# First weights of experts 4 to 30 in 4 MB transfers with 32 KB runs, another issue order, and the last second weight in the first-weight ring

## The reference

```python
for e in range(N_EXPERTS):                       # 32 experts
    z = jnp.einsum('bsd,df->bsf', h, w1[e]) + b1[e]      # w1[e]: 1024 x 2048 float32, 8 MB
    glu = jnp.minimum(z[..., 0::2], SWIGLU_LIMIT)
    lin = jnp.clip(z[..., 1::2], -SWIGLU_LIMIT, SWIGLU_LIMIT)
    act = glu * jax.nn.sigmoid(SWIGLU_ALPHA * glu) * (lin + 1.0)
    out = out + combine[..., e:e + 1] * (jnp.einsum('bsf,fd->bsd', act, w2[e]) + b2[e])   # w2[e]: 1024 x 1024, 4 MB
```

## Time and profile before

| | |
|---|---|
| median of 3 executions | 1123.79 us (1121.34 to 1123.82) |
| profiled execution | 1121.74 us, its span 1120.0 us |
| mean granted clock of TensorE | 0.985 of 2.4 GHz |
| TensorE matmuls busy | 1050.3 us (94%) |
| moved from HBM | 427.98 MB, 384 GB/s over the span |
| queue of SP's transfers | 40180 packets, 427.34 MB, 91.3% of 16 engines' span |
| chain of waits | PE 67%, DMA 30% |

### The profile page before, as it was taken

How to read it: one execution, slowest core, us unless ns; L and a number is a source line. 1 busy time by engine, 2 the same in 40 slices (tenths; PEclk the granted TensorE clock), 3 DMA queues, 4 the chain that set the end, 5 groups by cost and what they waited for, 6 DMA issues and landing times.

```text
span 1120.0 us, 11962 instructions
## 1 busy us (share of the span) xinstructions
PE 1050.3 (94%) x4658; PEld 406.7 (36%) x4658; DVE 288.7 (26%) x694; ACT 181.6 (16%) x323; POOL 17.4 (2%) x20
## 2 busy tenths in 40 slices
PE   8899998999999999998999999898989898989895
PEld 7548644333333333332333323232323232323231
DVE  3446345122222222121221212221212131312122
ACT  3411133111111111111111111111111111111102
POOL 0320000000000000000000000000000000000000
PEclk8999998999999999999999999999999999999998
DMA  9773592999899999999999999999999999999984
GB/s 303 218 273 150 224 411 102 367 427 425 369 430 425 427 427 430 430 427 428 430 430 428 427 430 430 428 427 428 430 430 427 428 430 430 427 427 430 428 365 189
DMA packets 41833, 430.89 MB, mean 385 GB/s; under 512 B 5856, under 2 KB 7444, under 8 KB 17012
## 3 DMA queue, kind: packets, MB, share of 16 engines
q1 hardware_dynamic: 40180, 427.34, 91.3%
q10 hardware_dynamic: 1216, 1.70, 0.8%
q0 software_dynamic: 416, 1.57, 0.4%
HBM read 427.98 MB, written 2.62 MB: 384 GB/s over the span
## 4 chain that ended last, share of the span: by engine, by line
PE 67%; DMA 30%; DVE 2%; SPq 1%; issue 1%; ACT 0%; DVEq 0%; ACTq 0%
DMA w1r<-w_mlp 28%; PE ps L1097 27%; PE ps L1126 13%; PE ps L1142 5%; PE ps L909 5%; PE ps L921 4%; PE ps L1071 3%; PE ps L1003 1%; PE ps L1032 1%; PE ps L1079 1%; PE ps L1105 1%; DMA w2r<-w_mlp 1%; PE ps L1150 1%; DMA arena<-rel_bias 0%; PE ps L1088 0%
## 5 line engine op out<-in xcount | busy, mean ns | idle before, releaser
L1097 PE MATMUL ps<-w1r,arena 128*64 128x512 f32 x2048 | 475.2, 598 | 20.4 <-DMA w1r<-w_mlp 20.4
L1126 PE MATMUL ps<-w2r,arena 128*64 128x512 f32 x1024 | 230.1, 598 | 24.8 <-DMA w2r<-w_mlp 24.8
L1097 PEld LDWEIGHTS ps<-w1r,arena 128*64 128x64 f32 x2048 | 135.2, 136 | 280.9 <-issue 236.2
L1126 PEld LDWEIGHTS ps<-w2r,arena 128*64 128x64 f32 x1024 | 71.9, 137 | 172.5 <-issue 128.5
L830 DVE TENSOR_TENSOR acc<-ps,acc 128x512 f32<-128x512 f32 x64 | 41.2, 686 | 206.3 <-PE ps L1142 206.3
L822 DVE TENSOR_TENSOR arena<-arena 128x512 f32<-128x512 f32 x32 | 22.2, 693 | 199.1 <-ACT arena L509 199.0
L518 ACT ACTIVATE arena<-ps 64x512 f32<-64x512 f32 x32 | 18.9, 592 | 328.9 <-PE ps L1126 328.9
L788 DVE TENSOR_SCALAR sel_z<-small 96x64 bf16 (+1 forms) x32 | 6.1, 190 | 233.6 <-PE ps L1097 233.6
L1142 PE MATMUL ps<-arena 128*128 128x512 f32 x128 | 63.2, 618 | 1.3 <-ACT arena L520 1.3
L1071 PE MATMUL ps<-h,arena 128*64 128x512 f32 x256 | 62.1, 607 | 1.8 <-DVE arena L790 1.8
L909 PE MATMUL ps<-w1r,h 128*128 128x512 f32 x128 | 56.9, 603 | 0.0
(11 more groups left out here) (205 smaller groups left out, 544.0 us busy)
## 6 DMA issues: line engine op xcount, KB each, us to landing
w1r<-w_mlp SPq DMA_DIRECT2D x127, 2048.0 KB, 32.7
w2r<-w_mlp SPq DMA_DIRECT2D x64, 2048.0 KB, 23.4
w1r<-w_in SPq DMA_DIRECT2D x7, 2048.0 KB, 21.3
w1r<-w_out SPq DMA_DIRECT2D x2, 2048.0 KB, 10.0
w1r<-w_mlp SPq DMA_DIRECT2D x2, 1024.0 KB, 5.6
rel_table<-arena ACTq DMA_DIRECT2D x1, 1536.0 KB
acc<-x SPq DMA_DIRECT2D x2, 512.0 KB, 4.4
arena<-rel_table POOLq DMA_DIRECT2D x1, 1024.0 KB, 12.1
```

The lines of the kernel that those rows point to most:

```text
L1097: ins = mm(ps[64 * c:64 * c + 64, 2 * par + n, :], hgT[:, par, k % 4, 64 * (k // 4):64 * (k // 4) + 64], w1r[:, 8 * par + k, at:at + 512], ...
L1126: ins = mm(ps[at:at + 64, 4 + c, :], actT[:, k % 4, 64 * (k // 4):64 * (k // 4) + 64], w2r[:, k // 2, col:col + 512], start=False, stop=(k ...
```

## The change

- `HALVES = 14`, four semaphores `w1_half` and three `w2_last` are added.
- `next_half` replaces `next_w1` for experts 4 to 30: two transfers of 4 MB, four ring rows each, 32 KB in one piece per partition in HBM and in the ring (`w1_c`; the assignment of weight rows to partitions and ring rows is the same as before). The first waits until rows 0 to 3 of the expert two back are used, the second for rows 4 to 7. On TensorE, `z_rows` of these experts waits at k = 0 and k = 4 instead of at every even k. Experts 0 to 3 and 31 keep the 2 MB transfers.
- The order in `rest_of_sweep` becomes: w1 of 2, w1 of 3; then for m = 2, 3, 4: w2 of 2m-3, w1 of 2m, w2 of 2m-2, w1 of 2m+1; then w2 of 7; then for m = 5 to 14: w2 of 2m-2, w1 of 2m, w2 of 2m-1, w1 of 2m+1, with the pass of m = 15 written out, w1 of 31 in quarters, w2 of 30, and `last_w2`.
- `last_w2` puts w2 of expert 31 into ring rows 0 to 3 (expert 30's, rows 0 to 3) and not into `w2r`: one transfer of 2 MB as soon as rows 0 and 1 are used, and two of 1 MB (8 KB per partition) as soon as rows 2 and 3 are. `down(31)` waits for them at k = 0, 4 and 6.
- The final gain and the result move to ring rows 4 and 5.
- On TensorE steps 2 and 3 are written out; the loop runs over m = 2 to 14.
- Further sweeps get one more wait and other counts; they don't run here.

```diff
+            def next_half(base, e, par):
+                for h in range(2):
+                    sp.wait_ge(w1_used, 8 * base + (8 * (e - 2) + 4 * h + 4))
+                    at = 8 * par + 4 * h
+                    sp.dma_start(w1r[:, at:at + 4, :].rearrange("p a f -> p (a f)"), w1_c[e, h]).then_inc(w1_half[2 * par + h], 16)
+
+            def last_w2(base):
+                sp.wait_ge(w1_used, 8 * base + 8 * (NE - 2) + 2)
+                sp.dma_start(w1r[:, 0:2, :].rearrange("p a f -> p (a f)"), w2_v[NE - 1, 0]).then_inc(w2_last[0], 16)
+                sp.wait_ge(w1_used, 8 * base + 8 * (NE - 2) + 4)
+                for i in range(2):
+                    sp.dma_start(w1r[:, 2 + i, :], w2_v[NE - 1, 1, :, 2048 * i:2048 * i + 2048]).then_inc(w2_last[1 + i], 16)
+
                 next_w1(base, 2, 0)
                 next_w1(base, 3, 1)
-                next_w2(base, 1)
-                next_w1(base, 4, 0, range(0, 2))
-                next_w2(base, 2)
-                next_w1(base, 4, 0, range(2, 4))
-                next_w1(base, 5, 1, range(0, 1))
-                next_w2(base, 3)
-                next_w1(base, 5, 1, range(1, 4))
-                next_w2(base, 4)
-                with sp.Fori(3, NE // 2) as m:
-                    next_w1(base, 2 * m, 0)
+                with sp.Fori(2, 5) as m:
+                    next_w2(base, 2 * m - 3)
+                    next_half(base, 2 * m, 0)
+                    next_w2(base, 2 * m - 2)
+                    next_half(base, 2 * m + 1, 1)
+                next_w2(base, 7)
+                with sp.Fori(5, NE // 2 - 1) as m:
+                    next_w2(base, 2 * m - 2)
+                    next_half(base, 2 * m, 0)
                     next_w2(base, 2 * m - 1)
-                    next_w1(base, 2 * m + 1, 1)
-                    next_w2(base, 2 * m)
-                next_w2(base, NE - 1)
+                    next_half(base, 2 * m + 1, 1)
+                next_w2(base, NE - 4)
+                next_half(base, NE - 2, 0)
+                next_w2(base, NE - 3)
+                next_w1(base, NE - 1, 1)
+                next_w2(base, NE - 2)
+                last_w2(base)
...
-                if k % 2 == 0:
+                if halves and k % 4 == 0:
+                    pe.wait_ge(w1_half[2 * par + k // 4], 16 * lap)
+                if not halves and k % 2 == 0:
                     pe.wait_ge(w1_in[4 * par + k // 2], 16 * lap)
...
-                    if k % 4 == 0:
-                        pe.wait_ge(w2_in[k // 4], 16 * base + 16 * (e + 1))
+                    if last and k in (0, 4, 6):
+                        pe.wait_ge(w2_last[max(0, k // 2 - 1)], hb + 16)
+                    if not last and k % 4 == 0:
+                        pe.wait_ge(w2_in[k // 4], 16 * wb + 16 * (e + 1))
...
-                                 w2r[:, k // 2, col:col + 512], start=False, stop=(k == 7))
+                                 (w1r if last else w2r)[:, k // 2, col:col + 512], start=False, stop=(k == 7))
```

More of the change, by code:

```diff
@@ L32 @@
 SLOTS = 64
+HALVES = 14
 SWEEPS = S // SLOTS
@@ L170, in hybrid_block @@
         actT = carve(arena, 5376, [4, P])
-        fgb = w1r[:, 0, 0:1024]
-        res = w1r[:, 1:2, :].rearrange("p a (t d) -> p (a t) d", t=TT)
+        fgb = w1r[:, 4, 0:1024]
+        res = w1r[:, 5:6, :].rearrange("p a (t d) -> p (a t) d", t=TT)
         ps = ctx.enter_context(nc.psum_tensor("ps", [P, 8, 512], F32))
@@ L205, in hybrid_block @@
         w1_in = [sem(f"w1_in{i}") for i in range(8)]
+        w1_half = [sem(f"w1_half{i}") for i in range(4)]
         w1_first = sem("w1_first")
         w2_in = [sem(f"w2_in{i}") for i in range(2)]
+        w2_last = [sem(f"w2_last{i}") for i in range(3)]
         w1_used = sem("w1_used"); w2_used = sem("w2_used")
@@ L222, in hybrid_block @@
         w1_v = w_mlp1[0].rearrange("e (c p i a) f -> e c i p (a f)", c=2, p=P, i=2)
+        w1_c = w_mlp1[0].rearrange("e (c p j) f -> e c p (j f)", c=2, p=P)
         w2_v = w_mlp2[0].rearrange("e (c p j) d -> e c p (j d)", c=2, p=P)
@@ L328, in _ @@
                     base = sp.snap(r * NE)
+                    sp.wait_ge(w2_used, 4 * base)
                     next_w1(base, 0, 0)
@@ L1088, in z_bias, with z_rows @@
                         mm(ps[64 * c:64 * c + 64, 2 * par + n, :], sel_z[:, par, :], bias3[:, at:at + 512], start=True, stop=False)
-            def z_rows(base, lap, k, par):
-                if k % 2 == 0:
+            def z_rows(base, lap, k, par, halves):
+                if halves and k % 4 == 0:
+                    pe.wait_ge(w1_half[2 * par + k // 4], 16 * lap)
+                if not halves and k % 2 == 0:
                     pe.wait_ge(w1_in[4 * par + k // 2], 16 * lap)
@@ L1109, in hgT_until, with down @@
                 return min(e + 3, NE) if isinstance(e, int) else e + 3
-            def down(base, e, par, free=True, tail=False):
+            def down(base, hb, wb, e, par, free=True, tail=False, last=False):
                 pe.wait_ge(actT_sb, base + e + 1)
@@ L1151, in gates_T, with step @@
                 ins.then_inc(gT_tr, 1)
-            def step(base, hb, m, par, first=False, last=False):
+            def step(base, hb, wb, rb, m, par, first=False, last=False):
                 e = 2 * m + par
-                lap = hb + m + 1
+                halves = not (isinstance(m, int) and (m < 2 or last and par == 1))
+                if halves:
+                    lap = rb * (HALVES - par) + m - 1
+                else:
+                    lap = rb * (2 + par) + min(m + 1, 3)
                 head, tail = first and par == 0, last and par == 1
@@ L1160, in step @@
                 z_bias(base, e, par, free=not first)
-                z_rows(base, lap, 0, par)
-                z_rows(base, lap, 1, par)
+                z_rows(base, lap, 0, par, halves)
+                z_rows(base, lap, 1, par, halves)
                 if not tail:
@@ L1166, in step @@
                     gather(base, e + 1, 1 - par)
-                z_rows(base, lap, 2, par)
+                z_rows(base, lap, 2, par, halves)
                 if par == 1 and not first:
                     scatter(base, hb, m - 1, 0)
-                z_rows(base, lap, 3, par)
+                z_rows(base, lap, 3, par, halves)
                 if not tail:
                     gather_T(base, e + 1)
-                z_rows(base, lap, 4, par)
+                z_rows(base, lap, 4, par, halves)
                 if par == 1 and not first:
                     scatter(base, hb, m - 1, 1)
-                z_rows(base, lap, 5, par)
+                z_rows(base, lap, 5, par, halves)
                 if not head:
                     act_T(base, e - 1)
-                z_rows(base, lap, 6, par)
+                z_rows(base, lap, 6, par, halves)
                 if par == 1:
                     gates_T(base, hb, m)
-                z_rows(base, lap, 7, par)
+                z_rows(base, lap, 7, par, halves)
                 if not head:
@@ L1185, in step, with sweep @@
                         pe.wait_ge(added[1], hb + m)
-                    down(base, e - 1, 1 - par, free=not (first and par == 1), tail=tail)
-            def sweep(base, hb, start=False):
+                    down(base, hb, wb, e - 1, 1 - par, free=not (first and par == 1), tail=tail)
+            def sweep(base, hb, wb, rb, start=False):
                 gather(base, 0, 0)
@@ L1194, in sweep @@
                 gather_T(base, 0)
[L1195 to L1199, removed]
+                step(base, hb, wb, rb, 0, 0, first=True)
+                step(base, hb, wb, rb, 0, 1, first=True)
+                step(base, hb, wb, rb, 1, 0)
+                step(base, hb, wb, rb, 1, 1)
+                with pe.Fori(2, NE // 2 - 1) as m:
+                    step(base, hb, wb, rb, m, 0)
+                    step(base, hb, wb, rb, m, 1)
                 m = NE // 2 - 1
-                step(base, hb, m, 0)
-                step(base, hb, m, 1, last=True)
-                down(base, NE - 1, 1)
+                step(base, hb, wb, rb, m, 0)
+                step(base, hb, wb, rb, m, 1, last=True)
+                down(base, hb, wb, NE - 1, 1, last=True)
                 scatter(base, hb, NE // 2 - 1, 0)
                 scatter(base, hb, NE // 2 - 1, 1, bank=0)
-            sweep(0, 0, start=True)
+            sweep(0, 0, 0, 0, start=True)
             pe.wait_ge(sweeps_ready, 1)
@@ L1211, in _ @@
                 with pe.Fori(1, n) as r:
-                    sweep(pe.snap(r * NE), pe.snap(r * (NE // 2)))
+                    sweep(pe.snap(r * NE), pe.snap(r * (NE // 2)), pe.snap(r * (NE - 1)), r)
 _INS = ["x", "norm1_gain", "w_in", "rel_bias", "idx_k_ln_gain", "idx_k_ln_bias", "ret_gn_gain", "w_out",
```

## The result

The changed kernel takes 1115.99 us (median of 5, 1114.53 to 1116.48) against 1123.79 before; the ratio is 0.9935, with a 95% interval of 0.9921 to 0.9949. Its profiled execution took 1114.76 us with a span of 1113.0, where the one before took 1121.74 and 1120.0: 7.0 us less. The forecast was 9.5 less and 1113, most likely 1110 to 1116, and the measured median lies at the upper edge of that.

What follows compares the result with a forecast made beforehand. The prediction took the DMA transfers to bound the kernel from about 200 us. Its terms, -4.3 - 3.8 + 2.9 - 4.3 = -9.5 us, gave 1112.2 from 1121.74; it forecast 1113, most likely 1110 to 1116, range 1107 to 1120.

Steps and rivals of the forecast that it cites:

- What binds: Steady stage: from about 200 us transfers set the end; TensorE alone would take 53.76 us a pair instead of 58.74.
- Part 1: End of the kernel: w2 of expert 31 in free ring rows lets down(31) end earlier, -4.3 us (range 2.5 to 5).
- Part 2: Order of transfers: gap at 284 to 290 us goes, -3.8 us; new gaps near 426 and 457 us cost +2.9.
- Part 3: Steady stage: waiting for 4 MB instead of 2 gathers idle time into one 5 us wait a pair, 0 us.
- Part 4: First weights of experts 4 to 30: 32 KB runs, 432 runs fewer per engine at 10 ns, -4.3 us.
- Sum: Whole kernel: -4.3 - 3.8 + 2.9 - 4.3 = -9.5 us, 1112.2 us for an execution like the profiled one.
- the cut of the runs: First-weight transfers: runs are cut at 16 KB and 32 KB saves nothing; 1116.5 or 1118.6 us; chance 0.22.
- a slower byte: First-weight transfers: 32 KB runs are slower by the byte; 1123 to 1125 us at 1.2%; chance 0.10.
- The clock: Steady stage: an idle stretch per pair halves TensorE's clock and makes it the bound; 1147 us at five spells; chance 0.04.
- the rival of longer new gaps: New order: the new gaps near 426 and 457 us cost up to 6 us; 1116 us; chance 0.04.

Runs made afterwards that it cites:

- experiment 1: The kernel before with only the last second weight moved into ring rows 0 to 3 (final gain and result moved too); 1118.73 us, ratio 0.9971.
- experiment 2: The kernel before with the new order and the last second weight in the ring, first weights in 2 MB quarters with 16 KB runs; 1119.26 us, ratio 0.9978.
- experiment 6: The changed kernel with the order around expert 10 shifted, first-weight transfers between w2 of 7, 8 and 9; 1112.34 us, ratio 0.9898.
- experiment 5: The kernel with new order, last weight in the ring and quarters, its order around expert 10 shifted to separate w2 of 7, 8 and 9; 1114.93 us, ratio 0.9925.
- experiment 3: The changed kernel with each 4 MB half issued as two 2 MB transfers of 16 KB runs, coarse waits kept; 1119.13 us, ratio 0.9975.
- experiment 7: The changed kernel with the order around expert 10 shifted and w1 of experts 29 and 30 in quarters with fine waits; 1113.88 us, ratio 0.9912.
- experiment 4: The changed kernel with w1 of experts 29 and 30 in 2 MB quarters, waited for in quarters; 1116.28 us, ratio 0.9952.
- experiment 8: The kernel before with w1 of experts 6 to 30 in 4 MB transfers of 32 KB runs, waited for by halves; 1119.87 us, ratio 0.9974.

## Why the prediction was right, and where it was off

- **What binds**: right. All of the gain is in the transfers and in the end behind them; TensorE's busy time went up by 6.4 us and the kernel became faster.
- **Part 1, the last second weight, -4.3**: right. -4.3 behind X, alone (experiment 1) and in the changed kernel, and the reason given holds: TensorE, not the landing, is the late one (`down(31)` starts 1.9 us after `down(30)` and never waits for a transfer).
- **Part 2, the order, -3.8 + 2.9**: the step that was mis-sized. Both gaps came where they were put, at 426 and 458 us, behind w2 of 7 and 8, but they cost 2.6 + 1.5 = 4.1 in the changed kernel where 1.7 and 1.2 were forecast, and in quarters one gap costs 4.8. Forecast for the whole part: -0.9; by the traces 0.0 (experiment 2 against 1), and with the two fills of the buffer apart the gap's price comes back, 3.2 to 3.7 (experiments 6 and 5). Two things were left out of the ledger. The 32 KB runs of experts 4 to 9 were put into the sum but not into the ledger of part 2: 6 x 16 runs at 10 ns let the queue run empty 1.0 us sooner, while TensorE's time stays. The windows agree: by their bytes the queue runs empty at 425.6 in the changed kernel, and 1.1 us later, counted from S, with 16 KB runs (426.9, experiment 3). And the halved clock after the wait for w2 of 7 (1.7 us later) stood only in the bounds; it came in experiments 2, 3, 5 and 7 and not in the profiled executions of the changed kernel and of experiments 4 and 6, though the wait was of much the same length (2.98 and 2.99 us in these three, 3.03 to 3.25 in the others).
- **Part 3, coarse waits, 0**: right as far as can be told; 0.4 us (experiment 3 against 2), within what two traces of one code differ by. The one wait per pair is there, up to 4.1 us instead of 5, because the halved clock, which I had as a rival, takes part of the rest. It costs some 1.7 to 3.0 us of TensorE's time in a pair (groups of 5.35 and, at 889.78, 6.64 us instead of 3.65) and is hidden by the slack of 5, as the rival's own account said one or two spells would be.
- **Part 4, 32 KB runs, -4.3**: the price was right, 10 ns a run against 10 forecast, and the extrapolation from 2 KB and 16 KB runs held. It was an extrapolation beyond every size that a row showed, and the other row with 2 KB runs gave 32 ns, so that the choice between the two fell right is in part luck. In the whole it is 3.7 (experiment 3). Why it is not 4.3 is open: a gap made longer by the runs isn't the reason that the windows show, since by bytes the gaps cost 4.1 us in the changed kernel and 4.7 with 16 KB runs. The Trainium skill, "DMA: Bandwidth & Descriptors", section "Where 436 GB/s comes from", had led to an estimate of 9.5 ns and 4.1 us; the trace agrees with it on the price, 10 ns, and the steady rate, 430.8 GB/s, stays below that section's 435.2. The same section also says that for loads from HBM a lower limit binds, some 358 GB/s for a core; this trace, at 430.8, does not bear that out.
- **Sum**: -4.3 - 3.8 + 4.1 + 0.4 - 3.7 = -7.3, measured -7.2 from S to the end. The rest to the forecast's -9.5 is part 2 (1.2), part 4 (0.6) and part 3 (0.4). Only the first of these three is clearly more than traces of the same code differ by, and the sum mixes gaps by bytes with differences of traces, so its agreement to 0.1 us is partly chance. A small slip besides: 2 MB in 4.895 us is 428.4 GB/s, not 428.5; nothing hangs on it.
- **Rivals**: the cut of the runs is out by the packets, and it and a slower byte by 58.42. The clock happened and didn't bind. What came true beside the forecast is the rival of longer new gaps, though at 4.1 us and not at its 6.

Open: why S differs by up to 3.6 us between executions of the same code, and what decides whether a given idle stretch of 1.9 to 3.3 us halves the clock.

## What to carry to other kernels

Where one queue binds, keep a ledger of it, transfer by transfer: when each is wanted, when its buffer is free, and how long a restart takes, with every gain of the change already in it. A single buffer that is filled twice in a row needs other transfers between the two fills, to cover the time from landing to release and the restart; here 4 MB, some 10 us, were enough but for about half a microsecond. The reordering that took one stall away here moved such a pair somewhere else, so look for it there. Put the last transfer of a stream into a buffer that is already free.

## What the runs showed of the hardware

- With half as many runs for the same bytes, each run saved was worth 10 ns, from 16 KB to 32 KB (58.73 us a pair in experiment 3, 58.42 after), and the prediction's estimate from 2 KB and 16 KB runs was 10 ns too. The steady rate goes from 428.4 to 12 x 2.097 / 58.42 = 430.8 GB/s.
- TensorE's granted clock fell to half after idle stretches from 1.94 us (before 890.70, experiment 8) to 4.17 us (before 714.54, experiment 4), and once after 1.92 with a short bias behind it (experiment 7). It didn't fall after others as long: 2.00 us (before 1055.99, experiment 2), 2.98 us (the row below, after) and 3.25 us (before 366.28, experiment 2). So between 1.9 and 3.3 us the length alone doesn't tell. Nor did it fall after the same 1.92 in the seven other kernels with the last weight in the ring. Behind a wait for the first weight with the halved clock, a group of 16 matmuls took 5.0 to 6.7 us instead of 3.65.

```profile
422.88 3.65 PE L1152 MATMUL ps<-w2r,arena 128*64 128x512 f32 x16 [2.98 <-DMA w2r<-w_mlp]
```

- The stage before the experts took 195.0 to 198.6 us in ten executions, one of each kernel, though its program lines are the same in all ten.
